# A two-block sequence model on one core: transposes on 64-row halves, mask and maximum in one instruction, weight slots split in quarter pieces, the gate as a second factor

## The reference

```python
def masked_softmax(s, mask):                       # first block, 8 heads
    s = jnp.where(mask, s.astype(jnp.float32), -jnp.inf)
    m = jnp.max(s, axis=-1, keepdims=True)
...
    e = jnp.exp(s - m)
    d = jnp.sum(e, axis=-1, keepdims=True)
    return e / jnp.where(d > 0, d, 1.0)
...
        return gb[..., 0:1] * o_cmp + gb[..., 1:2] * o_slc + gb[..., 2:3] * o_win
...
def rg_lru(x, w_r, b_r, w_i, b_i, lam, reverse):   # second block
    r = sigmoid(block_diag(x, w_r, b_r)); i = sigmoid(block_diag(x, w_i, b_i))
    log_a = -RG_C * r * softplus(-lam)
    u = sqrt(-expm1(2.0 * log_a)) * (i * x)
    _, h = lax.associative_scan(_lin_combine, (exp(log_a), u), axis=1, reverse=reverse)
...
def neighbourhood_attention(q, k, v, rpb):         # second block, 16 heads of 64
...
        s = jnp.einsum('bqhd,bwqkhd->bhqwk', q_r, k_win).astype(jnp.float32) * scale
        s = s + bias
        p = jax.nn.softmax(s.reshape(B, H, GRID_W, win_r * WIN_C), axis=-1)
        return jnp.einsum('bhqwk,bwqkhd->bqhd', p, v_win)
...
    proj = h @ w_in[l]
    xa, za, q, k, v, zb, ga, gb = jnp.split(proj, split_pts, axis=-1)
```

## Time and profile before

| | us |
|---|---|
| median of three runs | 2107.45 |
| lowest, highest | 2106.59, 2108.77 |
| the profiled execution | 2111.28 |
| its span | 2109.5 |
| TensorE busy | 1940.0 (92%) |
| VectorE busy | 1261.9 (60%) |
| GpSimd busy | 1262.8 (60%) |
| ScalarE busy | 615.7 (29%) |

### The profile page before, as it was taken

The page is one execution under the profiler, slowest core; times in us unless marked ns, Lnnn a source line. Parts: engine busy times, 40 slices in busy tenths (PEclk is TensorE's granted clock), DMA queues, the critical chain, the costliest instruction groups (busy, mean ns, idle before and its releaser), DMA issues.

```text
span 2109.5 us, 27159 instructions
## 1 busy us (share of the span) xinstructions
PE 1940.0 (92%) x9830; PEld 1502.5 (71%) x9830; DVE 1261.9 (60%) x1654; ACT 615.7 (29%) x1116; POOL 1262.8 (60%) x560
## 2 busy tenths in 40 slices
PE   6998789999999989988899999996879999989997
PEld 4676557888888766755678888884667777768775
DVE  5866886476266458578575714655946766750353
ACT  4214662210011121266531100113025565550111
POOL 6443017788888754411278978884655555557773
PEclk8999989999999989988999999998999999999998
DMA  5232003343334212300123432542222223312221
GB/s 198 62 96 75 11 11 100 103 143 102 100 126 124 99 60 71 110 21 21 33 84 113 140 98 92 156 118 66 70 65 82 85 80 87 84 60 90 90 90 40
DMA packets 68676, 182.39 MB, mean 86 GB/s; under 512 B 23888, under 2 KB 24144, under 8 KB 68432
## 3 DMA queue, kind: packets, MB, share of 16 engines
q1 hardware_dynamic: 60480, 154.48, 23.7%
q10 hardware_dynamic: 8080, 26.32, 3.9%
HBM read 178.67 MB, written 2.10 MB: 86 GB/s over the span
## 4 chain that ended last, share of the span: by engine, by line
PE 66%; DVE 20%; ACT 8%; issue 4%; DMA 1%; ACTq 0%; DVEq 0%
PE PS L392 20%; PE PS L396 19%; PE PS L395 19%; DVE tmp L1362 2%; DVE xc L1889 2%; DVE a_lo L1389 2%; ACT P L1230 1%; PE PS L681 1%; PE PS L431 1%; PE PS L643 1%; PE PS L631 1%; DVE PS L1599 1%; DVE rg L1950 1%; ACT rg L1301 1%; DVE rg L1944 1%
## 5 line engine op out<-in xcount | busy, mean ns | idle before, releaser
L2052 POOL TENSOR_TENSOR w_hi<-raw,const 128x1024 fp32r<-128x1024 f32 x278 | 559.8, 2014 | 791.2 <-PE PS L392 783.9
L392 PE MATMUL PS<-a_hi,w_hi 128*128 128x512 f32 x1616 | 657.6, 407 | 73.8 <-DVE a_lo L1389 18.9
L2054 POOL TENSOR_TENSOR w_lo<-raw,w_hi 128x1024 fp32r<-128x1024 f32 x278 | 702.9, 2528 | 21.8
L395 PE MATMUL PS<-a_lo,w_hi 128*128 128x512 f32 x1616 | 639.1, 396 | 0.0
L396 PE MATMUL PS<-a_hi,w_lo 128*128 128x512 f32 x1616 | 638.5, 395 | 0.0
L392 PEld LDWEIGHTS PS<-a_hi,w_hi 128*128 128x128 f32 x1616 | 309.2, 191 | 165.1 <-issue 42.2
L396 PEld LDWEIGHTS PS<-a_hi,w_lo 128*128 128x128 f32 x1616 | 309.2, 191 | 67.2
L395 PEld LDWEIGHTS PS<-a_lo,w_hi 128*128 128x128 f32 x1616 | 309.9, 192 | 64.8 <-issue 3.7
L1773 DVE TENSOR_TENSOR work<-PS,rstd 128x512 f32<-128x512 f32 x88 | 60.9, 692 | 150.5 <-PE PS L396 142.2
L392 PE MATMUL PS<-f_hi,w_hi 128*128 128x512 f32 x352 | 138.7, 394 | 0.0
L396 PE MATMUL PS<-f_hi,w_lo 128*128 128x512 f32 x352 | 138.0, 392 | 0.0
(11 more groups left out here) (291 smaller groups left out, 2605.9 us busy)
## 6 DMA issues: line engine op xcount, KB each, us to landing
raw<-weights SPq DMA_DIRECT2D x278, 512.0 KB, 3.5
work<-mod_w ACTq DMA_DIRECT2D x24, 512.0 KB, 3.5
work<-cmp_w ACTq DMA_DIRECT2D x8, 1024.0 KB, 5.4
bias<-rpb SPq DMA_DIRECT2D x256, 12.0 KB
rgw<-rgw ACTq DMA_DIRECT2D x8, 256.0 KB, 2.9
out<-xc SPq DMA_DIRECT2D x8, 256.0 KB, 2.1
const<-const SPq DMA_DIRECT2D x1, 1436.5 KB, 15.1
x<-x_t SPq DMA_DIRECT2D x4, 256.0 KB, 7.0
```

Source lines behind the costliest of these rows:

```text
L392: ins = nc.tensor.matmul(out, wh, hi, start=start, stop=False)
L395: nc.tensor.matmul(out, wh, lo, start=False, stop=False)
L2052: G.tensor_tensor(w_hi[:, r, :, :], raw[:, r, :, :], ones, ALU.mult).then_inc(pool_chain, 1)
L2054: G.tensor_tensor(w_lo[:, r, :, :], raw[:, r, :, :], w_hi[:, r, :, :].bitcast(F32), ALU.subtract)\
```

## The change

Four things are altered.

1. **Transposes of the second block** (`turn_values`, `near_turn`). Each transposes a 64-row half of the partitions (64x128 in, 128x64 out, with the 64x64 corner of the identity) where it was 128x128. The two halves alternate and go to two banks: head 0 and 1 of the values to banks 7 and 4, queries 0 to 63 and 64 to 127 of the softmax rows to banks 4 and 5. All sixteen of the values stand behind product q; the second half stood behind product k. Copies and `near_values` address the new layout.
2. **Mask and maximum** (`near_maxima`). Mask addition, negation and minimum are one instruction per head and block, 128x256, four in all. `max_ok` is raised once per head instead of once in all; `near_exps` waits per head and scales by -1.
3. **Quarter pieces** (`split`). In turns of the ring with an input projection of the first block, the first two gate slots of a layer, or a slot of the second block up to its loop's end, GpSimd writes `w_hi` in four instructions of 128x256 and then `w_lo` in four. Other turns stay as they are. The one loop becomes several, with straight code between.
4. **The gate** (`scale`, first block). The 128x2 product of reciprocal and gate is gone; the scaling of the rows has the gate as its second factor.

GpSimd, one slot in the loop over turns of the ring: before,

The diff, cut to its core:

```diff
--- before.py
+++ after.py
@@ -100,6 +100,16 @@
              + [(m, k) for m in range(OUT_EARLY, KT) for k in range(KT)])
+PIECES = 4
+def beside_vector(item):
+    if item[0] == "in2":
+        return item[1] < 6 * KT
+    return item[0] == "in" or item[0] == "gate" and item[2] < 2
 
@@ -783,15 +793,19 @@
 
-            def turn_values(p, half):
-                if claim(("vT", p, half), 7):
-                    pe.wait_ge(*room(("vT", p, half)))
-                for n in range(4):
-                    i, c = 2 * half + n // 2, n % 2
-                    k0 = LOW[i] * ROWS + c * P
-                    ins = nc.tensor.transpose(PS[:, 7, n * P:(n + 1) * P], qkv[:, p % 2, 2, k0:k0 + P], ident)
-                ins.then_inc(filling(("vT", p, half))[0], 1)
+            def turn_values(p):
+                for hh in range(2):
+                    if claim(("vT", p, hh), (7, 4)[hh]):
+                        pe.wait_ge(*room(("vT", p, hh)))
+                for n in range(8):
+                    k0 = LOW[n // 2] * ROWS + n % 2 * P
+                    for hh in range(2):
+                        r = slice(HD * hh, HD * hh + HD)
+                        ins = nc.tensor.transpose(PS[:, (7, 4)[hh], n * HD:(n + 1) * HD], qkv[r, p % 2, 2, k0:k0 + P],
+                                                  ident[r, r])
+                        if n == 7:
+                            ins.then_inc(filling(("vT", p, hh))[0], 1)
 
@@ -812,13 +826,16 @@
                 pe.wait_ge(scaled.sem, scaled.seen_by("pe"))
-                for hh in range(2):
-                    if claim(("PT2", u, hh), 4 + hh):
-                        pe.wait_ge(*room(("PT2", u, hh)))
-                    for n in range(4):
-                        ins = nc.tensor.transpose(PS[:, 4 + hh, n * P:(n + 1) * P],
-                                                  P2[:, 2 * hh + n // 2, n % 2 * P:(n % 2 + 1) * P], ident)
-                    ins.then_inc(filling(("PT2", u, hh))[0], 1)
+                for r in range(2):
+                    if claim(("PT2", u, r), 4 + r):
+                        pe.wait_ge(*room(("PT2", u, r)))
+                for n in range(8):
+                    for r in range(2):
+                        q = slice(HD * r, HD * r + HD)
+                        ins = nc.tensor.transpose(PS[:, 4 + r, n * HD:(n + 1) * HD],
+                                                  P2[q, n // 2, n % 2 * P:(n % 2 + 1) * P], ident[q, q])
+                        if n == 7:
+                            ins.then_inc(filling(("PT2", u, r))[0], 1)
 
@@ -826,16 +843,20 @@
                         pe.wait_ge(*room(("O2", p)))
-                pe.wait_ge(*emptying(("vT", p, half)))
-                for hh in range(2):
-                    pe.wait_ge(*emptying(("PT2", u, hh)))
+                if half == 0:
+                    for hh in range(2):
+                        pe.wait_ge(*emptying(("vT", p, hh)))
+                for r in range(2):
+                    pe.wait_ge(*emptying(("PT2", u, r)))
+                turned = PT2[:, :, :].rearrange("p (r a) b -> p r (a b)", r=2)
                 for n in range(2):
...
                             ins = nc.tensor.matmul(PS[p0:p0 + HD, 6, i * P:(i + 1) * P], vW[:, 2 * i + c, p0:p0 + HD],
-                                                   PT2[:, 2 * hh + n, c * P:(c + 1) * P], start=c == 0, stop=c == 1)
+                                                   turned[:, :, (4 * hh + 2 * n + c) * HD:(4 * hh + 2 * n + c + 1) * HD],
+                                                   start=c == 0, stop=c == 1)
                 if half == 0:
@@ -855,10 +876,9 @@
                         pe.wait_ge(*emptying(("v", p)))
-                        turn_values(p, 0)
+                        turn_values(p)
                         near_scores(2 * p)
                     elif p >= 0 and part == "k":
-                        turn_values(p, 1)
                         near_scores(2 * p + 1)
@@ -1222,12 +1242,13 @@
             def near_exps(u):
-                act.wait_ge(max_ok.sem, max_ok.seen_by("act"))
                 if u:
...
                 for i in range(4):
-                    ins = A(P2[:, i, :], PS[:, 2 + i // 2, i % 2 * 256:(i % 2 + 1) * 256], ACT.Exp,
+                    if i % 2 == 0:
+                        act.wait_ge(max_ok.sem, max_ok.seen_by("act"))
+                    ins = A(P2[:, i, :], PS[:, 2 + i // 2, i % 2 * 256:(i % 2 + 1) * 256], ACT.Exp, scale=-1.0,
                             bias=sm2[:, i:i + 1], accum_out=sm2[:, 4 + i:5 + i])
@@ -1257,7 +1278,7 @@
                     act.wait_ge(*filling(("vT", p, 0)))
-                    A(vW[:, 0:4, :], PS[:, 7, :].rearrange("p (n c) -> p n c", c=P), ACT.Copy)\
+                    A(vW[:, :, 0:HD], PS[:, 7, :].rearrange("p (n c) -> p n c", c=HD), ACT.Copy)\
                         .then_inc(emptied(("vT", p, 0)), 1)
@@ -1642,11 +1663,10 @@
                     dve.wait_ge(dve_chain.sem, dve_chain.raised())
-                    TT(r3[:, 0:2], r3[:, 0:2], gN[:, i, both:both + BR + 1:BR], ALU.mult).then_inc(dve_chain.sem, 1)
-                    dve.wait_ge(dve_chain.sem, dve_chain.raised())
                     for hh in range(2):
                         pr = work[:, 2 * br + hh, 0:w]
-                        TS(pr, pr, r3[:, hh:hh + 1], None, ALU.mult).then_inc(scaled.sem, 1)
+                        gate = gN[:, i, both + BR * hh:both + BR * hh + 1]
+                        TS(pr, pr, r3[:, hh:hh + 1], gate, ALU.mult, ALU.mult).then_inc(scaled.sem, 1)
                         dve.wait_ge(scaled.sem, scaled.raised())
@@ -1906,15 +1926,17 @@
                     dve.wait_ge(dve_chain.sem, dve_chain.raised())
-                for n in range(2):
-                    i = 2 * half + n
-                    s = PS[:, 2:4, n * 256:(n + 1) * 256].rearrange("p b (c r) -> p b c r", r=ROWS)
-                    mask = nm[:, i, :].unsqueeze(1).unsqueeze(3).to_broadcast([P, 2, KC, ROWS])
-                    TT(s, s, mask, ALU.add).then_inc(dve_chain.sem, 1)
-                    dve.wait_ge(dve_chain.sem, dve_chain.raised())
-                V.tensor_reduce(sm2[:, 0:4], PS[:, 2:4, :].rearrange("p b (n c) -> p (b n) c", c=256), AX.X, ALU.max,
-                                negate=True).then_inc(max_ok.sem, 1)
-                dve.wait_ge(max_ok.sem, max_ok.raised())
+                for hh in range(2):
+                    for n in range(2):
+                        s = PS[:, 2 + hh, n * 256:(n + 1) * 256].rearrange("p (c r) -> p c r", r=ROWS)
+                        mask = nm[:, 2 * half + n, :].unsqueeze(2).to_broadcast([P, KC, ROWS])
+                        ins = V.tensor_tensor_reduce(s, s, mask, -1.0, -2 * NEG_MASK, ALU.add, ALU.min,
+                                                     sm2[:, 2 * hh + n:2 * hh + n + 1])
+                        if n == 0:
+                            ins.then_inc(dve_chain.sem, 1)
+                            dve.wait_ge(dve_chain.sem, dve_chain.raised())
+                    ins.then_inc(max_ok.sem, 1)
+                    dve.wait_ge(max_ok.sem, max_ok.raised())
 
@@ -1965,7 +1987,7 @@
                     dve.wait_ge(*filling(("vT", p, 1)))
-                    CP(vW[:, 4:8, :], PS[:, 7, :].rearrange("p (n c) -> p n c", c=P))\
+                    CP(vW[:, :, HD:P], PS[:, 4, :].rearrange("p (n c) -> p n c", c=HD))\
                         .then_inc(emptied(("vT", p, 1)), 1)
@@ -2044,26 +2066,47 @@
 
-            def split(r, arrival, used, chain):
+            ones = c_("ones")[:, 0:1].unsqueeze(2).to_broadcast([P, 8, P])
+            def split(r, arrival, used, chain, pieces):
 
...
                     pool.wait_ge(slot_used, used)
-                G.tensor_tensor(w_hi[:, r, :, :], raw[:, r, :, :], ones, ALU.mult).then_inc(pool_chain, 1)
-                pool.wait_ge(pool_chain, chain)
-                G.tensor_tensor(w_lo[:, r, :, :], raw[:, r, :, :], w_hi[:, r, :, :].bitcast(F32), ALU.subtract)\
-                    .then_inc(split_done, 1)
-            ones = c_("ones")[:, 0:1].unsqueeze(2).to_broadcast([P, 8, P])
+                each = 8 // pieces
+                for n in range(pieces):
+                    k = slice(n * each, (n + 1) * each)
+                    G.tensor_tensor(w_hi[:, r, k, :], raw[:, r, k, :], ones[:, k, :], ALU.mult).then_inc(pool_chain, 1)
+                for n in range(pieces):
+                    k = slice(n * each, (n + 1) * each)
+                    pool.wait_ge(pool_chain, chain + n + 1)
+                    ins = G.tensor_tensor(w_lo[:, r, k, :], raw[:, r, k, :], w_hi[:, r, k, :].bitcast(F32), ALU.subtract)
+                ins.then_inc(split_done, 1)
+            def pieces_of(turn):
+                return PIECES if any(beside_vector(item) for item in PLAN[turn * RING:(turn + 1) * RING]) else 1
             pool.wait_ge(head_in, 16)
-            for r in range(RING):
-                split(r, 16, None, r + 1)
-            with pool.Fori(1, SLOTS // RING) as i:
```

(26 more changed lines are left out.)

## The result

The changed kernel takes 2051.6 us (median of four runs, 2050.0 to 2054.6) against 2107.0 (2105.5 to 2108.8): a ratio of 0.974, 95% interval 0.972 to 0.976. That is 55.4 us faster, where 34 were forecast; the time lies in the range, 1.6 us above its lower end of 2050. The profiled execution has a span of 2052.6 us.

The account below looks back on a forecast made before the run. VectorE and GpSimd excluding each other on SBUF was taken to stand behind most TensorE waits. Terms 5 + 6 + 9 + 8 + 6 = 34 us gave 2077.3 profiled, 2073.5 as median; range 2050 to 2097.

Parts of the forecast that it names:

- signs of being wrong: Pieces over 0.75 us, a VectorE instruction still over 2 us beside them, or TensorE waiting for `split_done`.
- signs of being right: Convolution additions 1.1 to 1.2 us, pieces 0.5 to 0.65, loop period 1 us shorter, L1649's waits below 20 us, among others.
- slower rival: "Pieces cost more, slower": each further piece adds 0.25 us, +21, 2128 us; border at 0.17 us a piece; chance 0.09.
- Start: Start of the kernel: VectorE instructions lose less to pieces, but slot 0 is split later; -5 us (-2 to -6.3).
- Projections: Projection stages: quarters remove TensorE's two waits of 3.4 us behind VectorE; -6 us (-3 to -9).
- Convolution: Second block's convolution stage: less excess on VectorE; -9 us (0 to -14.3, the latter if each instruction meets one piece only).
- Loop: Loop over head pairs: quarters shorten the ring through ScalarE and VectorE by 1.0 us per pair; -8 us (-4 to -12).
- that cover stays: Mask and maximum, loop: ScalarE stays busy with gates until after the maximum is ready; term zero (0 to -2 us).
- The case of 1.6 us per set: Half-array transposes: sixteen loads cost twice today's unless halves load together; loss 1.5 us per pair, 12 in all, 2093.
- Gate: First block: dropping the 128x2 product saves 0.25 us where TensorE waits for L1649; -6 us (-2 to -11).
- No gap between the pieces: Rival: GpSimd's pieces overlap, so VectorE waits for all four as now; only the gate term stands, 2103 us; chance 0.13.
- contention returns elsewhere: Rival inside the forecast's own range: convolution and loop give 0 and 4 us since GpSimd's total is unchanged, 2090 us.

Follow-up runs that it names:

- with the pause: Changed kernel, but a slot's first w_lo piece waits for all four w_hi pieces, so GpSimd pauses once per slot: 2039.9 us, ratio 0.968.

## Why the prediction was right, and where its steps failed

**The number.** 2051.6 lies inside the range, but far from its centre of 2073.5, and that it stayed inside is in part luck: 15.4 of the 55.4 us come from stages that the sum had left at zero. Two of its signs of being wrong came true in a small way: VectorE instructions of over 2 us beside pieces (the starved ones, in a kernel that is faster all the same), and TensorE waiting for splits (14.1 us in 3 times, 10.8 in one before). One of its signs of being right didn't come: the waits of L1649 are 21.7 us, not below 20. What follows goes through the steps.

**What bounds the kernel.** Right: VectorE and GpSimd exclude each other on SBUF, and that contention, much more than the second block's transposes or mask, was what the change was worth. Trace and runs agree (48 us for the pieces alone).

**Price of a piece.** Taken 0.57 us with 0.035 for a further instruction; the rows without VectorE beside them:

```profile
28.05 2.33 POOL L2079 TENSOR_TENSOR w_hi<-raw,const 128x256 fp32r<-128x256 f32 x4
30.34 2.82 POOL L2083 TENSOR_TENSOR w_lo<-raw,w_hi 128x256 fp32r<-128x256 f32 x4
```

From start to start that is 2.29 and 2.78, 0.57 and 0.70 a piece, 0.64 in the mean: my upper bound. A further piece costs 0.13 us, since the whole ones took 1.89 and 2.39. The slower rival's border of 0.17 was worked out for eight further pieces per slot, where quarters make only six; with six it is 0.23. So four pieces are clear of it. Eight pieces have its slot (6.2 us, 6.3 in the rival) and its mechanism in the convolution stage, but not its size: 2085 us, not 2128, and a loop that is 4 us longer than with four pieces, not 25.

**Loss of a VectorE instruction.** Taken 0.4 us for each piece, 56 of them in the convolution. The additions took 1.05 us, so 0.29 each, the products 0.11: 24 x 0.29 + 8 x 0.11 = 8 us lost, and 22 of the 30 came back, not 7.9. The step that failed is "56 pieces x 0.4 = 22.4 us": where it isn't starved, an instruction meets one piece at most, so instructions have to be counted, not pieces. That was the alternative in the sum (14.3), and with 0.29 for 0.4 even it was low. The page "SBUF — State Buffer" of the Trainium skill says in its section "Who interferes with whom" that the first to issue holds the pair for its whole instruction. The trace agrees only in part. A 0.76 us addition and a piece of 0.57 or 0.70 us together take 1.0 to 1.1 us where they alternate, so part of the two runs side by side. And the starved instruction, issued at 41.95, was passed by pieces that were issued up to 57.74, so the order of issue didn't decide there.

**Start**, -5: 31.8 to 25.4, -6.4. Right, but lost again to the starved instruction.

**Projections**, -6: -11.0 in layer 1 and, with the pause, 93.0 to 83.5 in layer 0. Under-sized: the two waits of 3.4 us were counted, but the waits for issue behind them (3.0 us per layer) and the clock were not. In layer 1 idle time fell from 11.4 to 5.2 us and busy time from 90.7 to 85.9, at a granted clock of 0.92 and then 0.96; some 2 of the 11.0 can be chance, as said above.

**Output stages and feed-forward edges**, not in the sum: -15.4 together. This is the largest omission, and it stood in the profile of before:

```profile
PE PS L392 <- DVE a_lo L1389: 18.9, 8, 4.1
```

After it is 2.3 us in 3 waits. I had taken four waits from that list and left out its second longest. The feed-forward network behind it gains by the clock too. The rows below are 350 to 400 us, first before, then after. Before, TensorE idled 3.5 us up to 370.9, in the output stage. In the network's first 29 us it was then busy throughout, and its mean granted clock was still 0.92, between the levels of 1.2 and 2.4 GHz. After, it is busy throughout and at 2.4 GHz:

```profile
350.00:400.00 50.00, 46.47 (x189) 36.76 (x188) 31.56 (x27) 13.76 (x18) 35.27 (x16) 0.93 0.32 103
```

```profile
350.00:400.00 50.00, 50.00 (x220) 40.84 (x219) 23.84 (x26) 13.38 (x17) 46.83 (x32) 1.00 0.39 124
```

**Convolution**, -9: -20.7, of which 3 come back at the entry of the loop (the first `near_scores` comes 29.2 us after the first q before, 32.2 after). Without these 17.7, still twice the term, for the reason above.

**Loop**, -8: the size of the effect per pair was right, its cause only in part. A steady pair went from 39.42 to 38.45 us, 0.97 where 1.0 stood. With the pieces alone it is 39.25, with the transposes alone 39.31: 0.17 and 0.11, not 1.0 and 0. The step that failed is "that cover stays" under mask and maximum. The cover was thin. In the kernel before the maximum is over at 1621.38, and ScalarE starts the exponentials at 1621.59, 0.2 us later:

```profile
1620.16 1.22 DVE L1915 TENSOR_REDUCE sm<-PS 128x4 f32<-128x1024 f32 x1
1621.59 0.47 ACT L1230 ACTIVATE P<-PS,sm 128x256 f32<-128x256 f32 x1
```

With the pieces ScalarE is no longer late, and the maximum is. ScalarE's and VectorE's timelines of the pieces alone:

```profile
1613.85 0.48 ACT L1240 ACTIVATE P<-PS,sm 128x256 f32<-128x256 f32 x1 [0.78 <-DVE sm L1925]
```

```profile
1612.54 1.22 DVE L1925 TENSOR_REDUCE sm<-PS 128x4 f32<-128x1024 f32 x1
```

In the changed kernel ScalarE goes from the vW copy to the first exponential without idling. The kernel without pieces, which has mask and transposes, takes 39.31 per pair, no less than the transposes alone, and waits as long as they do:

```profile
PE PS L820 <- ACT P L1251: 10.2, 7, 1.5
```

So without pieces the fused mask adds nothing; pieces and transposes do little alone, and all three bring about 1 us per pair together. How the 0.8 us that mask and transposes bring on top of the pieces divide between the two wasn't run apart. Over the loop only 1.5 us show, since the two starved instructions of 5.2 us lie in the second pair (41.3 us against 37.8 for the third and 38.5 for the others) and the convolution's 3 us land here; with one pause it takes 326.6 us.

**Transposes**: a set of sixteen, from its start to the next product, takes 0.64 us (forecast 0.6), and TensorE's own path per pair (period less wait) went from 38.47 to 37.81, 0.66 less where 0.6 stood:

```profile
1618.50 0.71 PE L835 MATMUL PS<-const,P 64*128 64x64 f32 x16
1619.14 0.50 PE L402 MATMUL PS<-a_hi,w_hi 128*128 128x512 f32 x1
```

The case of 1.6 us per set is out. The text was at odds with itself on one sign: by its sum the wait had to fall to 0.54 us (0.94 + 0.6 - 1.0), while the list of signs said "not shorter". It is 0.64 in a steady pair.

**Gate**, -6: 5.7 alone (3 to 8.4). Right, within that.

**Rivals.** "No gap between the pieces" had the fact right (each starts 0.04 us before the profile has the last one end) and the result wrong in most places, right in a few, and there it costs 5 to 17 us at once. The trace agrees so far with the rule that the prediction quotes from the page "GPSIMD Engine Reference" of the Trainium skill, section "Instruction dispatch". "Pieces cost more" and "contention returns elsewhere" are out: convolution and loop together gave 22.2 us.

## What to carry to other kernels

Where VectorE and GpSimd share SBUF, cutting GpSimd's instructions short brought 48 us here, and a wait on the engine's own last instruction, once per weight slot, another 12 at no cost that shows. Cut no finer than the engine has time for: with eight pieces, and with pieces and a pause for every slot, TensorE waited for the splits. Count the victim's instructions, not the pieces, and read the whole list of waits before putting a number on the gain. Where several engines end a wait within half a microsecond of each other (0.2 us here), edits that bring nothing alone can bring a microsecond together, so a cover has to be looked at again with the rest of the change in place.

## What the runs showed of the hardware

A VectorE instruction can be kept waiting by a long row of GpSimd instructions that follow each other without a pause: 26 pieces and 16.55 us in the changed kernel, 27.9 us and some 40 pieces with pieces everywhere. Mostly it gets in at the next boundary: in the same kernel all the instructions of the start and the convolution did, though each piece there too starts 0.04 us before the last one ends. Some starved ones get in between two pieces after several have passed (the 5.23 us one in the loop ended at 1537.10, while the row went on), others only when the row ends. What decides isn't settled. It isn't the instruction's size or form (a 128x8 scaling and a 128x512 addition both starved), and none starved in the four kernels where GpSimd paused for 0.08 us at least once per slot.
